# Second block of a two-block transformer on one core: compression chunks placed between projection chunks, gate and `v` columns in shared products, blank tiles cleared by POOL, compressed softmax ahead of a weight split

## The reference, cut to what matters

```python
h = rms_norm_2(x, g_pre_mix)
u, v, q, kv, nsa_g, xr, rg, mg = split(h @ w_in)
k_cmp, v_cmp, k_slc, v_slc, k_win, v_win = split(kv, 6)
y_a = gelu(u) * (w_s @ layer_norm(gelu(v)) + b_s)
# nsa mixer: 15 blocks of 32 positions, stride 16, 4 groups of 64 columns
kc = gelu(flat(blocks(k_cmp) + pe_k) @ wk1) @ wk2
vc = gelu(flat(blocks(v_cmp) + pe_v) @ wv1) @ wv2
p_c = softmax(q @ kc.T * scale, masked);  o_cmp = p_c @ vc
g = sigmoid(nsa_g)                        # 48 columns
y_b = g0 * o_cmp + g1 * o_slc + g2 * o_win
y_c = rglru(xr, rg)
x = x + rms_norm_2((gates0 * (y_a @ w_a) + gates1 * (y_b @ w_b) + gates2 * (y_c @ w_c)) @ w_o)
x = x + rms_norm_2((silu(f_gate) * f_up) @ w_ffn_out)
```

## Time and profile before

| what | value |
|---|---|
| median of 3 runs | 1367.68 us (1365.34 to 1367.81) |
| the profiled execution's own time | 1364.43 us |
| its span | 1362.7 us |
| mean granted clock of TensorE | 0.969 of full |
| PE busy, chain's share | 1289.5 us (95%), 80% |
| DVE busy, chain's share | 851.0 us (62%), 12% |
| ACT busy, chain's share | 649.6 us (48%), 3% |
| POOL busy | 145.0 us (11%) |
| HBM read | 211.8 MB, 156 GB/s over the span |

### The profile page before, as it was taken

The page is one execution under the profiler, slowest core; times in us unless marked ns, Lnnn a source line. Parts: engine busy times, 40 slices in busy tenths (PEclk is TensorE's granted clock), DMA queues, the critical chain, the costliest instruction groups (busy, mean ns, idle before and its releaser), DMA issues.

```text
span 1362.7 us, 16993 instructions
## 1 busy us (share of the span) xinstructions
PE 1289.5 (95%) x6498; PEld 1080.4 (79%) x6498; DVE 851.0 (62%) x1015; ACT 649.6 (48%) x938; POOL 145.0 (11%) x161
## 2 busy tenths in 40 slices
PE   6979799999997989999999989989999999899998
PEld 5868788888886878888888878778998778688886
DVE  4688765555567886555446572766786686555544
ACT  4455454444444563544445352645464754544444
POOL 2928000000066430000000000000000000000000
PEclk9989899999988989999999998999999999899999
DMA  6512356555352314555554452333324445465551
GB/s 226 184 63 93 109 183 217 185 185 201 112 203 107 124 58 153 209 189 186 190 189 179 175 189 106 121 142 109 124 93 155 154 175 189 146 216 185 185 202 61
DMA packets 33962, 213.66 MB, mean 157 GB/s; under 512 B 4304, under 2 KB 6352, under 8 KB 9584
## 3 DMA queue, kind: packets, MB, share of 16 engines
q1 hardware_dynamic: 33840, 212.73, 43.7%
q0 software_dynamic: 64, 0.13, 0.0%
HBM read 211.80 MB, written 1.05 MB: 156 GB/s over the span
## 4 chain that ended last, share of the span: by engine, by line
PE 80%; DVE 12%; ACT 3%; POOL 2%; issue 2%; DMA 0%; DVEq 0%; SPq 0%; ACTq 0%; POOLq 0%
PE bank L534 23%; PE bank L535 23%; PE bank L536 23%; PE bank L868 3%; DVE wlo L1527 2%; PE bank L675 2%; PE bank L643 2%; PE bank L662 1%; PE bank L562 1%; ACT whi L1094 1%; PE bank L749 1%; DVE nmax L1656 1%; DVE index L1615 1%; DVE probs L1651 1%; DVE z L2008 1%
## 5 line engine op out<-in xcount | busy, mean ns | idle before, releaser
L1527 DVE TENSOR_TENSOR wlo<-raw,whi 128x2048 fp32r<-128x2048 f32 (+2 forms) x202 | 450.7, 2237 | 244.8 <-ACT whi L1094 243.2
L534 PE MATMUL bank<-whi,hT_hi 128*128 128x512 f32 (+2 forms) x1040 | 417.2, 401 | 13.9 <-DVE hT_lo L1551 6.1
L1094 ACT ACTIVATE whi<-raw 128x2048 fp32r<-128x2048 f32 (+2 forms) x202 | 370.5, 1840 | 109.4 <-PE bank L536 107.5
L535 PE MATMUL bank<-wlo,hT_hi 128*128 128x512 f32 (+2 forms) x1040 | 408.3, 393 | 0.0
L536 PE MATMUL bank<-whi,hT_lo 128*128 128x512 f32 (+2 forms) x1040 | 407.6, 392 | 0.0
L534 PEld LDWEIGHTS bank<-whi,hT_hi 128*128 128x128 f32 x1040 | 201.6, 194 | 56.9 <-DVE wlo L1527 9.1
L536 PEld LDWEIGHTS bank<-whi,hT_lo 128*128 128x128 f32 x1040 | 201.2, 193 | 41.8
L535 PEld LDWEIGHTS bank<-wlo,hT_hi 128*128 128x128 f32 x1040 | 201.6, 194 | 37.8
L534 PE MATMUL bank<-whi,mixT_hi 128*128 128x512 f32 (+1 forms) x248 | 96.0, 387 | 7.2 <-DVE mixT_lo L1551 4.6
L535 PE MATMUL bank<-wlo,mixT_hi 128*128 128x512 f32 (+1 forms) x248 | 93.9, 379 | 0.0
L536 PE MATMUL bank<-whi,mixT_lo 128*128 128x512 f32 (+1 forms) x248 | 93.9, 379 | 0.0
(11 more groups left out here) (259 smaller groups left out, 1432.4 us busy)
## 6 DMA issues: line engine op xcount, KB each, us to landing
raw<-in_ff_loop SPq DMA_DIRECT2D x90, 1024.0 KB, 4.8
raw<-in_w_groups SPq DMA_DIRECT2D x77, 1024.0 KB, 4.8
raw<-in_w_out SPq DMA_DIRECT2D x8, 1024.0 KB, 4.8
raw<-in_ff_first SPq DMA_DIRECT2D x6, 1024.0 KB, 4.8
raw<-in_w_comp SPq DMA_DIRECT2D x4, 1024.0 KB, 4.8
raw<-in_ff_last SPq DMA_DIRECT2D x3, 1024.0 KB, 6.5
raw<-in_next_first SPq DMA_DIRECT2D x4, 512.0 KB, 3.2
raw<-in_next_first SPq DMA_DIRECT2D x2, 1024.0 KB, 4.8
```

Of the source, the lines that this page charges most:

```text
L534: eng.matmul(out, lhsT=hi, rhs=wh, start=start, stop=False)
L535: eng.matmul(out, lhsT=hi, rhs=wl, start=False, stop=False)
L1094: eng.activation(whi[j][:, 0:n], raw[j][:, 0:n], ACT.Copy).then_inc(hi_ready, 1)
L1527: eng.tensor_tensor(wlo[j][:, 0:n], raw[j][:, 0:n], whi[j][:, 0:n].bitcast(F32), ALU.subtract).then_inc(lo_ready, 1)
```

## The change

ORDER2 gives the ring's new order of chunks, and SP, ACT, DVE and PE follow it. Product 4 is now 48 gate columns and 308 of `v` (356 columns), products 8 and 9 are 358 columns of `v` each, instead of 48, 512 and 512. The four compression chunks alternate with the chunks of products 4 and 5 and accumulate in banks 4 and 5. The splits of the flat blocks come ahead of the split of (4, 0). The three memsets go to POOL, each behind a semaphore. DVE's split of (10, 0) goes behind the last step of the compressed softmax. `attend_turn` of the first group goes between the row halves of (11, 1). The two halves of the row turn 7 stand around `group_values(1)`.

```diff
+V_CUTS = {4: (0, 308), 8: (308, 666), 9: (666, 1024)}
+ORDER2 = [(0, 0), (0, 0), (0, 1)] + [(b, j) for b in (1, 2, 3) for j in range(2)] + \
+    [(4, 0), (6, 0), (4, 1), (6, 1), (5, 0), (7, 0), (5, 1), (7, 1)] + [(b, j) for b in range(8, 30) for j in range(2)]
@@ SP
+            for i in range(3, CHUNKS2):
+                b, j = ORDER2[i]
+                load(T2, i, weights2(b)[j])
+                if (b, j) == (5, 1):
+                    next_gain(5, t["rows2"][0, :])
+                if (b, j) == (7, 1):
...
+                        eng.dma_start(z[:, v, KC2:KC2 + 512], t["w_gates"][v]).then_inc(rg_loaded, 16)
...
@@ POOL
+            eng.wait_ge(par_loaded, 64 * (LAYERS + 1))
+            eng.memset(headsT[:, T2_V:T2_V + 4, :], 0.0).then_inc(blank_ready, 1)
+            eng.wait_ge(filled, F_SK + 1)
+            eng.memset(scr[:, :, :], 0.0).then_inc(blank_ready, 1)
+            eng.wait_ge(filled, F_WK + 1)
+            eng.memset(probs[:, 0:2, :], 0.0).then_inc(blank_ready, 1)
@@ PE
+                bank_read = lambda r: eng.wait_ge(free[r], product(b) - (b == 8))
+                chunk(T2, chunk2(b, j), 4 * j, 4, width2(b), bank_read, between)
...
-                        mm = three(bank[v][0:COMP, 0:SEQ], 4 * c + k, slice(0, COMP), i % RING, k * COLS + v * SEQ,
+                        mm = three(bank[4 + v][0:COMP, 0:SEQ], 4 * c + k, slice(0, COMP), i % RING, k * COLS + v * SEQ,
...
-            product_chunk(4, 0, GATES); product_chunk(4, 1, GATES)
+            product_chunk(4, 0); compress(6, 0)
+            product_chunk(4, 1); compress(6, 1)
             product_chunk(5, 0)
             eng.wait_ge(dup_ready, 3)
             turn_four(lambda g, r: scr[:, r, g * P:(g + 1) * P], 4)
-            product_chunk(5, 1)
-            compress(6, 0); compress(6, 1)
+            compress(7, 0)
+            product_chunk(5, 1); compress(7, 1)
             eng.wait_ge(dup_ready, 4)
             turn_four(lambda g, r: probs[:, r, g * P:(g + 1) * P], 5)
-            compress(7, 0); compress(7, 1)
             product_chunk(8, 0)
...
-            attend_turn(A)
-            product_chunk(11, 1)
+            product_chunk(11, 1, between=lambda: attend_turn(A))
...
-            group_scores(2); group_values(1)
-            turn_rows(7, z[:, :, U2:U2 + D])
+            group_scores(2)
+            turn_half(7, 0, z[:, :, U2:U2 + D])
+            group_values(1)
+            turn_half(7, 1, z[:, :, U2:U2 + D])
+            eng.wait_ge(turned_lo, 32)
@@ ACT
-            hi2(4, 0); take(3, 0, z[:, 0, KS2:KS2 + COLS], ACT.Copy); hi2(4, 1)
+            eng.wait_ge(flat_done, 1)
+            eng.activation(flat[0].rearrange("p j m -> p (j m)"), flat_f, ACT.Copy).then_inc(flat_hi, 1)
+            hi2(4, 0); take(3, 0, z[:, 0, KS2:KS2 + COLS], ACT.Copy); hi2(6, 0)
             fill_copy(0, F_Q, 0)
             fill_copy(0, F_Q + 2, 4)
-            hi2(5, 0)
-            take(4, 0, z[:, 0, G2:G2 + GATES], ACT.Tanh, GATES, rs_half)
-            take(4, 1, z[:, 1, G2:G2 + GATES], ACT.Tanh, GATES, rs_half)
-            hi2(5, 1)
...
-            hi2(6, 0); fill_copy(0, F_SK, T2_KS); take(5, 0, z[:, 0, KW2:KW2 + COLS], ACT.Copy); hi2(6, 1)
-            hi2(7, 0); fill_copy(0, F_WK, T2_KW); hi2(7, 1)
-            hi2(8, 0)
+            hi2(4, 1); hi2(6, 1); hi2(5, 0)
+            eng.wait_ge(filled, F_Q + 3)
+            for r in range(RT):
+                whole(4, r)
+                act(eng.activation(z[:, r, G2:G2 + GATES], bank[r][:, 0:GATES], ACT.Tanh, scale=rs_half[:, r:r + 1]))
+                take_v(4, r, GATES)
+            hi2(7, 0); hi2(5, 1)
+            fill_copy(0, F_SK, T2_KS)
+            hi2(7, 1); take(5, 0, z[:, 0, KW2:KW2 + COLS], ACT.Copy)
+            hi2(8, 0); fill_copy(0, F_WK, T2_KW)
...
@@ DVE
-            lo2(4, 0); take1(3, z[:, 1, KS2:KS2 + COLS]); lo2(4, 1)
+            lo2(4, 0)
+            eng.wait_ge(flat_hi, 1)
+            eng.tensor_tensor(flat[1].rearrange("p j m -> p (j m)"), flat_f,
+                              flat[0].rearrange("p j m -> p (j m)").bitcast(F32), ALU.subtract).then_inc(flat_lo, 1)
+            take1(3, z[:, 1, KS2:KS2 + COLS])
+            fill_copy(F_Q + 1, 2)
+            fill_copy(F_Q + 3, 6)
+            lo2(6, 0)
             for r in range(RT):
                 eng.wait_ge(free[r], 4)
             twice(scr, KS2, 3)
-            fill_copy(F_Q + 1, 2)
-            fill_copy(F_Q + 3, 6)
-            lo2(5, 0)
...
-            lo2(5, 1)
+            lo2(4, 1); lo2(6, 1); lo2(5, 0); lo2(7, 0)
...
-            lo2(6, 0); fill_copy(F_SK + 1, T2_KS + 2); take1(5, z[:, 1, KW2:KW2 + COLS])
+            fill_copy(F_SK + 1, T2_KS + 2)
+            lo2(5, 1); lo2(7, 1); take1(5, z[:, 1, KW2:KW2 + COLS])
...
             twice(probs, KW2, 4)
-            lo2(6, 1)
-            lo2(7, 0); fill_copy(F_WK + 1, T2_KW + 2); lo2(7, 1)
-            eng.wait_ge(par_loaded, 64 * (LAYERS + 1))
-            dve(eng.memset(scr[:, :, :], 0.0))
-            dve(eng.memset(headsT[:, T2_V:T2_V + 4, :], 0.0))
-            dve(eng.memset(probs[:, 0:2, :], 0.0))
-            dve.wait(eng)
+            lo2(8, 0); fill_copy(F_WK + 1, T2_KW + 2)
...
-            lo2(8, 0); lo2(8, 1)
+            lo2(8, 1)
             lo2(9, 0)
             eng.wait_ge(read67[1], 7)
+            eng.wait_ge(blank_ready, 3)
...
-            lo2(10, 0)
             eng.wait_ge(ce_ready, 1)
...
                .then_inc(cn_ready, 1)
+            lo2(10, 0)
```

More of the change, by code:

```diff
@@ L241, in block_one_and_two @@
         pad_ready = sem("pad_ready")
+        blank_ready = sem("blank_ready")
         cs_ready = sem("cs_ready")
@@ L383, in _, with weights2 @@
                 load_first(t0, CHUNKS1, t["next_first"][l])
-            def load2(b, src):
-                for j in range(2):
-                    load(T2, chunk2(b, j), src[j])
+            def weights2(b):
+                if b in (4, 8, 9):
+                    return t["w2_gates_v"] if b == 4 else t["w2_v"][b - 8]
+                if b in (6, 7):
+                    return t["w2_comp"][b - 6]
+                return t["w2_groups"][b if b < 4 else 4 if b == 5 else b - 5]
             for dst, name in ((small[:, 0:416], "small2"), (par, "channel2")):
@@ L391, in _ @@
             eng.dma_start(w_s, t["w_s"]).then_inc(ws_loaded, 16)
[L392 to L411, removed]
+            for i in range(3, CHUNKS2):
[4 more added lines that the diff above has]
+                if (b, j) == (7, 1):
+                    eng.wait_ge(filled, F_CV + 1)
+                    for v in range(2):
+                        eng.dma_start(z[:, v, KC2:KC2 + 512], t["w_gates"][v]).then_inc(rg_loaded, 16)
+                if (b, j) == (12, 1):
+                    next_gain(6, t["rows2"][1, :])
+                if (b, j) == (15, 1):
+                    next_gain(7, t["rows2"][2, :])
             eng.wait_ge(xc_ready, 8)
@@ L594, in first_product @@
                 mm.then_inc(used, 1)
[L596 to L600, removed]
             def turn_heads(l, s, src, pairs):
@@ L878, in compress @@
                 if c == 0:
-                    for r in range(RT):
-                        eng.wait_ge(free[r], product(6))
                     eng.wait_ge(flat_lo, 1)
@@ L1297, in take, with take_v @@
                 eng.activation(dst, bank[r][:, 0:n], func, scale=scale[:, r:r + 1]).then_inc(free[r], 1)
+            def take_v(b, r, c0=0):
+                lo, hi = V_CUTS[b]
+                whole(b, r)
+                eng.activation(z[:, r, lo:hi], bank[r][:, c0:c0 + hi - lo], ACT.Gelu_apprx_tanh, scale=ssq[:, 4 + r:5 + r])\
+                   .then_inc(free[r], 1)
             def fill_copy(n, count, t0):
@@ L1414, in _ @@
             eng.activation(hidT, bank[7][:, 0:4 * COMP], ACT.Copy).then_inc(read67[1], 1)
-            eng.wait_ge(filled, F_Q + 3)
-            take(8, 0, z[:, 0, 0:COLS], ACT.Gelu_apprx_tanh)
-            take(8, 1, z[:, 1, 0:COLS], ACT.Gelu_apprx_tanh)
+            take_v(8, 0)
+            take_v(8, 1)
             hi2(9, 1)
@@ L1424, in _ @@
             hi2(10, 0)
-            take(9, 0, z[:, 0, COLS:D], ACT.Gelu_apprx_tanh)
-            take(9, 1, z[:, 1, COLS:D], ACT.Gelu_apprx_tanh)
+            take_v(9, 0)
+            take_v(9, 1)
             hi2(10, 1)
```

29 lines of the change are left out of this document (15 added, 14 removed).

## The result

The kernel after takes **1343.03 us** (median of 4 runs, 1342.15 to 1343.89) against 1366.51 us (1365.10 to 1367.81) for the kernel before on the same chip: ratio 0.9825, 95% interval [0.9813, 0.9836], 23.5 us less. Forecast were 1349.7 us, 18.0 us less, with a range from 1345. The sign is right. The profiled execution took 1342.15 us, its span is 1340.4 us (before 1362.7), the mean granted clock 0.975 (0.969), PE is busy 1276.6 us (1289.5), DVE 847.1 (851.0), ACT 649.3 (649.6). PE has 81% of the chain.

The account below looks back on a forecast made before the run. PE sets the pace, losing time before 930 us to holes (12.8 us idle) and low clock. Terms -11.0 - 1.65 - 2.5 + 0.25 - 1.95 - 1.1 = -18.0 us, from median 1367.68 to 1349.7; own range 1346 to 1354, with rivals 1345 to 1358.

Parts of the forecast that it names:

- fill wait: Last q transposes, ahead of (4, 0): their wait for DVE's copy goes as the copies come first, -0.6 us.
- part 1: From the q transposes to the start of (9, 0): holes filled, widths changed, clock kept up, -11.0 us with the fill wait.
- part 2: From (9, 0) to (10, 0): narrower (9, 0), -1.65 us, and softmax steps ahead of DVE's split of (10, 0), -2.5 us.
- part 3: attend_turn inside (11, 1): half of that chunk fills the turn's two holes of 1.31 us, -1.95 us.
- product 10's steps: DVE's steps for product 10 start later against PE, which waits for their last copies, +0.25 us.
- part 4: Turned rows: group_values(1) fills the hole of 1.07 us between the two halves, -1.1 us.
- (13, 0): Low clock behind the hole ahead of this chunk: loss of 1.7 us left in, bound 0 to -1.7.
- rival A: The new order keeps some of its holes, with low clock behind the largest: 1356.7 us, chance 0.22.
- C: Rival: the ring starves in the alternation, each chunk (4, 0) to (8, 1) with a 3.1 us hole: 1380.7 us, chance 0.03.
- E: Rival: an engine late behind 930 us eats the gain, no change, 1367.7 us, chance 0.02.
- rival D: Clock stays up in part 4 (-1.7 us) and falls 2 us later in the scores (-1): 1347.0 us, chance 0.08.
- the two clock prices: Clock losses behind holes: at (13, 0) bounded 0 to -1.7 us, in part 3 not counted.

Follow-up runs that it names:

- 1st before: The unchanged kernel before, in the profile that the prediction read; q transposes to attend_turn behind (13, 0) took 154.13 us, median 1366.51 us.
- 3rd before: The kernel before run again unchanged for one more profile; q transposes to attend_turn behind (13, 0) took 157.44 us.
- attend_alone: The kernel before with only attend_turn of group A moved inside (11, 1): 1359.77 us, ratio 0.9952 to the kernel before.
- the second: The kernel before run again unchanged, its second profile; q transposes to attend_turn behind (13, 0) took 157.48 us.

## Why the prediction was right or wrong

| step | forecast | 1st before to after | 3rd before to after |
|---|---|---|---|
| fill wait | -0.6 | -0.74 | -0.74 |
| part 1, (4, 0) to (9, 0) | -10.4 | -11.16 | -11.09 |
| part 2, to (10, 0) | -4.15 | -3.85 | -3.94 |
| part 3 and product 10's steps, to (12, 0) | -1.7 | -1.99 | -4.92 |
| part 4, holes | -1.1 | -1.31 | -1.66 |
| (13, 0) | 0 | -1.55 | -1.56 |
| sum | -17.95 | -20.60 | -23.91 |

**Right: the holes and what fills them.** Part 1's order keeps none of the holes (rival A is out), the ring feeds it (C), no clock falls from 773 to 820 us, and the hi split of (5, 0), forecast to wait for its load until about 783, waited until 781.3. The excess of 0.7 us is mostly two waits counted at 0.3 us and not there, and full products at 5.50 and 5.57 us instead of 5.65. Part 2: from (9, 1) to (10, 0) 7.35 us for 9.84, forecast 7.36; the split is the last to come there (ends 837.91, PE at 838.12). Part 3's own term: attend_alone, 40.12 to 38.15, 1.97 for 1.95; PE waits 1.00 and 0.69 us there, forecast 2. The +0.25 for product 10's steps doesn't show, its place is 38.15 without and 38.13 with it. Behind the stretch nothing was eaten (E).

**Wrong: the clock.** The step that failed is how stretches at 0.50 were counted. The prediction credited 3.5 us to the clock, 2.2 at (5, 0) and 1.3 at (8, 0), gave part 3 the length of its holes alone, 1.95 us, and left the loss at (13, 0) in ("the nearest row is the same place, so I leave the loss"). The runs show 34.1 us at 0.50 in the third profile of before (the second is within 0.1 us of it) and 13.7 in after. Against the third profile the parts give 6.0 us more than forecast, and 4.9 of these are falls that the sum had at nothing: 3.3 us for the two behind the holes of part 3, which the one profile didn't show and which attend_alone takes away, and 1.6 for the one at (13, 0). The other 1.1 us are small: 0.7 in part 1, 0.4 in the rest together. Part 1's own falls were in the durations that the prediction subtracted, and are no part of the miss.

The fall at (13, 0) was priced, as a bound and in rival D, and set at zero for a reason that the runs refute: the place was the same, but not what preceded it. attend_alone, which leaves the place as it was, removes it. D's other half, a fall 2 us later in the scores, didn't come: 2.6 us behind their start, before 2.8.

**The offset was not neutral.** The profiled execution lay 3.25 us under the median of three runs, and that was carried over to the forecast as it stood. Over 43 executions of the kernel before, time goes with the mean clock of TensorE: 1368.2 us at 0.967 (7 of them), 1366.9 at 0.968 (10), 1366.0 at 0.969 (23), 1362.4 to 1363.1 at 0.972 and 0.973 (3). The profiled execution is none of the three: it has 0.969, and was at 0.50 for 84 us of its span, just as long as the third profile. Only the places differ. By slices it had 6.8 us less of it in the stretch and 6.8 more in block 1. Busy time and clock from 20 to 100 us, the first profile and the third:

```profile
20.00:100.00 80.00, 72.35 (x351) 60.10 (x350) 57.10 (x85) 35.54 (x59) 42.78 (x40) 0.89 0.39 142
20.00:100.00 80.00, 72.35 (x364) 60.25 (x363) 58.50 (x85) 36.62 (x59) 42.84 (x40) 0.94 0.39 141
```

That cost it 1.85 us ahead of the q transposes (772.82 for 770.97) and spared it 3.3 in the stretch, where a change could have won them. Against the third profile the parts give 23.9 us, as the medians do (23.5).

**The range** ended at 1345 since the bounds of the two clock prices were 1.7 us and nothing for part 3. A term at nothing has a bound too: a hole of 1.31 us without a fall in one profile can have one in the next.

## What to carry to other kernels

A hole on TensorE costs its own length and, in some executions of this kernel, 1.5 to 1.7 us more for the clock behind it: before pricing an edit that fills holes, read two or three profiles of the same kernel and compare the granted clock behind each hole. Judge small edits by the starts of the same instructions around the place (repeatable to 0.1 us in after) rather than by the whole time, in which block 1's end alone lay anywhere from 770.7 to 774.0 us. A row of many tiny matmuls can be the dearest thing in sight although PE shows as fully busy: joining two of them along the contraction with zeros gave 6.1 us, more than any other edit to the kernel after.
